# Two groups of heads scored in one TensorE stage, in three of the five attention mixers of a float32 transformer kernel

## The reference, cut to what matters

```python
# differential attention (layers 0 and 3): 8 heads, each with two score maps j = 0, 1 of 64 dimensions
s = jnp.einsum('bqhjd,bkhjd->bhjqk', qb, k) * scale + bias
s = jnp.where(dist >= 0, s, NEG)
p = jax.nn.softmax(s, axis=-1)
a = p[:, :, 0] - lam_full * p[:, :, 1]
o = jnp.einsum('bhqk,bkhe->bqhe', a, v)

# stick-breaking attention (layer 1): 16 heads of 64 dimensions
z = jnp.einsum('bqhd,bkhd->bhqk', qb, k) * scale
log_1m_beta = jnp.where(strict, jax.nn.log_sigmoid(-z), 0.0)
between = lax.cumsum(log_1m_beta, axis=3, reverse=True) - log_1m_beta
a = jnp.where(strict, jnp.exp(jax.nn.log_sigmoid(z) + between), 0.0)

# block attention with ALiBi (second block): 8 heads of 64 dimensions; with 256 tokens
# a query sees its own block alone, so this is causal attention over all keys
p = jax.nn.softmax(where(kpos <= qpos, q @ k.T - slopes * (qpos - kpos), -inf), axis=-1)
# beside it, on the other half of the channels
y = jnp.einsum('bsgc,gcd->bsgd', trailing_mean(p_in) - p_in, pool_w)
```

## Time and profile before

| what | us |
|---|---|
| median of 3 runs | 1755.77 (1755.76 to 1756.32) |
| span of the profiled execution | 1753.6 |
| what lies around the span in the runs (median less span) | 2.2 |
| TensorE busy, matmuls | 1744.2 (99%) |
| VectorE busy | 1301.7 (74%) |
| ScalarE busy | 1059.2 (60%) |
| GpSimd busy | 97.1 (6%) |

### The profile page before, as it was taken

The page is one execution under the profiler, slowest core; times in us unless marked ns, Lnnn a source line. Parts: engine busy times, 40 slices in busy tenths (PEclk is TensorE's granted clock), DMA queues, the critical chain, the costliest instruction groups (busy, mean ns, idle before and its releaser), DMA issues.

```text
span 1753.6 us, 33156 instructions
## 1 busy us (share of the span) xinstructions
PE 1744.2 (99%) x13030; PEld 1646.4 (94%) x13030; DVE 1301.7 (74%) x1899; ACT 1059.2 (60%) x1592; POOL 97.1 (6%) x144
## 2 busy tenths in 40 slices
PE   9999999999999999999999999999999999999998
PEld 8999999999999999999999999999999999998887
DVE  7668878877877886877876697788666876556665
ACT  6776566666666666666666766566454555346444
POOL 3000000122000013000000000003000020000000
PEclk9999999999999999999999999999999999999999
DMA  9445555534566544565554465655555544435652
GB/s 310 147 145 168 193 191 159 190 133 138 176 203 190 180 170 146 170 214 181 180 179 145 146 192 192 187 183 193 192 180 195 161 164 139 161 127 189 201 178 96
DMA packets 238483, 306.27 MB, mean 175 GB/s; under 512 B 13763, under 2 KB 212981, under 8 KB 238333
## 3 DMA queue, kind: packets, MB, share of 16 engines
q1 hardware_dynamic: 236708, 300.27, 52.5%
q0 software_dynamic: 1552, 4.28, 0.7%
q10 hardware_dynamic: 104, 0.07, 0.0%
HBM read 303.53 MB, written 1.07 MB: 174 GB/s over the span
## 4 chain that ended last, share of the span: by engine, by line
PE 99%; DVE 0%; ACT 0%; issue 0%; DVEq 0%; POOL 0%; POOLq 0%; ACTq 0%
PE ps L1111 22%; PE ps L1112 22%; PE ps L1113 22%; PE ps L1467 17%; PE ps L1469 9%; PE ps L1278 1%; PE ps L1298 1%; PE ps L1625 0%; PE ps L1124 0%; PE ps L1328 0%; PE ps L1315 0%; PE ps L1270 0%; PE ps L1395 0%; PE ps L1353 0%; PE ps L1386 0%; PE ps L1367 0%
## 5 line engine op out<-in xcount | busy, mean ns | idle before, releaser
L1683 DVE TENSOR_TENSOR sb_w_lo<-sb_raw,sb_w_hi 128x2048 fp32r<-128x2048 f32 x283 | 646.0, 2290 | 225.4 <-ACT sb_w_hi L907 224.6
L907 ACT ACTIVATE sb_w_hi<-sb_raw 128x2048 fp32r<-128x2048 f32 x283 | 538.5, 1908 | 160.5 <-PE ps L1113 78.7
L1111 PE MATMUL ps<-sb_a_hl,sb_w_hi 128*128 128x256 f32 x1840 | 529.3, 288 | 1.8 <-DVE sb_a_hl L1697 1.0
L1112 PE MATMUL ps<-sb_a_hl,sb_w_hi 128*128 128x256 f32 x1840 | 520.4, 283 | 0.0
L1113 PE MATMUL ps<-sb_a_hl,sb_w_lo 128*128 128x256 f32 x1840 | 520.2, 283 | 0.0
L1467 PE MATMUL ps<-sb_a_hl,sb_w_hi 128*128 128x512 f32 x1280 | 447.6, 393 | 0.0
L1111 PEld LDWEIGHTS ps<-sb_a_hl,sb_w_hi 128*128 128x128 f32 x1840 | 352.2, 191 | 9.8 <-issue 6.4
L1469 PE MATMUL ps<-sb_a_hl,sb_w_lo 128*128 128x256 f32 x1280 | 358.2, 280 | 0.0
L1112 PEld LDWEIGHTS ps<-sb_a_hl,sb_w_hi 128*128 128x128 f32 x1840 | 352.5, 192 | 0.4
L1113 PEld LDWEIGHTS ps<-sb_a_hl,sb_w_lo 128*128 128x128 f32 x1840 | 352.4, 192 | 0.0
L1467 PEld LDWEIGHTS ps<-sb_a_hl,sb_w_hi 128*128 128x128 f32 x1280 | 239.7, 187 | 53.2
(11 more groups left out here) (264 smaller groups left out, 1908.9 us busy)
## 6 DMA issues: line engine op xcount, KB each, us to landing
sb_raw<-in_ffn_w_up SPq DMA_DIRECT2D x102, 1024.0 KB, 5.3
sb_raw<-in_ffn_w_down SPq DMA_DIRECT2D x66, 1024.0 KB, 4.9
sb_raw<-in_da_w_qkv SPq DMA_DIRECT2D x23, 1024.0 KB, 5.2
sb_raw<-in_ffn_w_gate SPq DMA_DIRECT2D x22, 1024.0 KB, 5.3
sb_raw<-in_w_o SPq DMA_DIRECT2D x16, 1024.0 KB, 5.0
sb_raw<-in_sb_w_qkv SPq DMA_DIRECT2D x12, 1024.0 KB, 5.2
sb_raw<-in_xa_wkv SPq DMA_DIRECT2D x8, 1024.0 KB, 5.4
sb_raw<-in_w_in SPq DMA_DIRECT2D x8, 1024.0 KB, 5.4
```

The source lines that it names most:

```text
L907: act.activation(w_hi[:, a % RING, :], raw[:, a % RING, :], ACT.Copy).then_inc(hi_ready, 1)
L1111: pe.matmul(o, hi1, hi2, start=start, stop=False, skip_group_check=True)
L1112: pe.matmul(o, hi1, lo2, start=False, stop=False, skip_group_check=True)
L1683: dve.tensor_tensor(w_lo[:, a % RING, :], raw[:, a % RING, :], w_hi[:, a % RING, :].bitcast(F32), ALU.subtract).then_inc(lo_ready, 1)
```

## The change

- `mix` on TensorE calls `scores` or `stick_scores` for groups g and g+1 one after the other, at the half where group g stood, for g = 0, 2, 4, 6 (differential, stick-breaking) or 0, 2 (block attention). The half that had group g+1 loses that stage. Sliding-window and cross attention stay as they are.
- Two groups need room: the wide part of group g goes to half g % 2 of bank 4 + head, the narrow part to a quarter of bank 2 + head (`score_tile`). `copy_scores` on VectorE thus becomes two instructions. VectorE waits for the scores of both groups before it reads the first.
- Bank 2 is no longer one of the projections': in these forms blocks 0, 1, 2 go to banks 0, 1, 6, and the rest turns over banks 0 and 1 (`proj_bank`), so block i waits for block i-2 to be taken. The norm's sum and its turned root move to bank 7.
- Bank 3 is now shared between narrow scores and what it held: `pool_mix(0)` waits for `biased` of groups 0 and 1; `back(0)` and the early `stick_values` wait for the first four groups to be read; the pair that starts with group 4 (group 2 in block attention) waits for `act_lo` to reach 4. The first output block begins with banks 2 and 3.
- The convolution's setup transposes move from banks 5 and 6 to 2 and 3.

```diff
+        def proj_bank(form, i):
+            if form in ("slide", "cross"):
+                return i % 3
+            return (0, 1, 6)[i] if i < 3 else (i - 3) % 2
+        def score_tile(form, g, s, wide_part):
+            if form == "slide":
+                return PS[:, 4 + s, P:3 * P] if wide_part else PS[:, 4 + s, 0:P]
+            if wide_part:
+                return PS[:, 4 + s, g % 2 * T:(g % 2 + 1) * T]
+            return PS[:, 2 + s, g % 2 * P:(g % 2 + 1) * P]
...
-                            pe.wait_ge(taken, ph["tk"] + i - 2)
+                            pe.wait_ge(taken, ph["tk"] + freed_block(form, i) + 1)
...
-                    if g >= 1:
+                    if g >= 1 and (form == "slide" or g % 2 == 0):
                         pe.wait_ge(biased, ph["sg"] + g)
+                    if form == "diff" and g == 4 or form == "moba" and g == 2:
+                        pe.wait_ge(act_lo[a], 8 * ph["out_fill"] + 4)
...
                         pe.wait_ge(rT_ready, rT_count[ph["n"]])
+                        pe.wait_ge(biased, ph["sg"] + 2)
...
-                        if h in at["scores"]:
+                        if h in at["scores"][::2]:
                             scores(at["scores"].index(h))
+                            scores(at["scores"].index(h) + 1)
...
-                    dve.wait_ge(scores_ready, sg + 1)
+                    dve.wait_ge(scores_ready, sg + (2 - g % 2 if form in ("diff", "moba") else 1))
...
-                    dve.wait_ge(z_done, g + 1)
+                    dve.wait_ge(z_done, g + 2 - g % 2)
...
-                    dve.tensor_scalar(of_group(zbuf, g), PS[:, 4:6, 0:3 * P], ph["scale"], None, ALU.mult)\
-                        .then_inc(z_copied, 1)
+                    z = of_group(zbuf, g)
+                    dve.tensor_scalar(z[:, :, 0:T], PS[:, 4:6, g % 2 * T:(g % 2 + 1) * T], ph["scale"], None,
+                                      ALU.mult)
+                    dve.tensor_scalar(z[:, :, T:3 * P], PS[:, 2:4, g % 2 * P:(g % 2 + 1) * P], ph["scale"], None, ALU.mult)                        .then_inc(z_copied, 1)
```

More of the change, by code:

```diff
@@ L414, in value_bank, with freed_block, root_bank, turned_root @@
             return 4 + g % 2
+        def proj_bank(form, i):
+            if form in ("slide", "cross"):
+                return i % 3
+            return (0, 1, 6)[i] if i < 3 else (i - 3) % 2
+        def freed_block(form, i):
+            return next(e for e in range(i - 1, -1, -1) if proj_bank(form, e) == proj_bank(form, i))
+        def root_bank(form):
+            return 3 if form in ("slide", "cross") else 7
+        def turned_root(form):
+            return DB[3][:, T:T + QB] if form == "slide" else PS[:, 7, 0:QB]
+        def score_tile(form, g, s, wide_part):
[4 more added lines that the diff above has]
+            return PS[:, 2 + s, g % 2 * P:(g % 2 + 1) * P]
         def heads_of(form, g):
@@ L1194, in project @@
                             pe.wait_ge(act_lo[ph["act"]], 8 * ph["fill"] + k + 1)
-                        o, first, js = PS[:, i % 3, j * T:(j + 1) * T], (j, k) == (0, 0), slice(j * P, (j + 1) * P)
+                        o, first, js = PS[:, proj_bank(form, i), j * T:(j + 1) * T], (j, k) == (0, 0), slice(j * P, (j + 1) * P)
                         if typ == "mv":
@@ L1230, in out_half @@
                     elif i == 0:
-                        order = [(k, m) for p in (2 * half, 2 * half + 1) for k in range(2) for m in (2 * p, 2 * p + 1)]
+                        pairs_of = (2 * half, 2 * half + 1) if form in ("slide", "cross") else ((2, 3), (1, 0))[half]
+                        order = [(k, m) for p in pairs_of for k in range(2) for m in (2 * p, 2 * p + 1)]
                     else:
@@ L1238, in out_half @@
                             pe.wait_ge(act_lo[a], 8 * ph["out_fill"] + arrival(form, c) + 1)
-                        if i == 0 and k == 0 and m in (0, 2, 4):
-                            pe.wait_ge(taken, ph["tk"] + max(n for n in range(N) if n % 3 == m // 2) + 1)
+                        if i == 0 and k == 0 and m == 4 and form == "stick":
+                            pe.wait_ge(z_copied, 8)
+                        elif i == 0 and k == 0 and m == 4 and form in ("diff", "moba"):
+                            pe.wait_ge(biased, ph["sg"] + ph["groups"])
+                        elif i == 0 and k == 0 and m in (0, 2, 4):
+                            pe.wait_ge(taken, ph["tk"] + max(n for n in range(N) if proj_bank(form, n) == m // 2) + 1)
                         if i == 0 and k == 0 and m == 6 and form in ("slide", "moba", "cross"):
@@ L1377, in stick_values @@
                     pe.wait_ge(a_ready, g + 1)
-                    if bank > 3:
-                        pe.wait_ge(z_copied, 8)
+                    pe.wait_ge(z_copied, 8 if bank > 3 else 4)
                     before = [e for e in range(g) if value_bank("stick", e) == bank]
@@ L1455, in mix @@
                             turn_probs(at["turn"].index(h))
-                        if h in at["scores"]:
+                        if form == "moba" and h in at["scores"][::2]:
+                            scores(at["scores"].index(h))
+                            scores(at["scores"].index(h) + 1)
+                        elif form != "moba" and h in at["scores"]:
                             scores(at["scores"].index(h))
```

38 lines of the change are left out of this document (22 added, 16 removed).

## The result

The change made the kernel slower by 0.13%, less than the 0.2% that I had said a measurement can tell; the interval of the ratio lies above 1.

The account below looks back on a forecast made before the run. TensorE was taken to bound the kernel. Fourteen joins at 0.40 us gain 5.6; waits of 2.5, 2.8 and 0.95 give +0.65, so the median goes from 1755.8 to 1756.4 us, range 1752.4 to 1759.5.

Parts of the forecast that it names:

- What bounds the kernel: TensorE, busy 1744.2 of 1753.6 us; only its own work and waits it does not have today can move the time.
- the 0.40 for leaving the 128-row form: Each second score group, put behind the first, saves 0.40 us of going from 128 rows to 64 and back.
- The gain of stick-breaking attention, 4 x 0.40: Four score pairs in stick-breaking attention each save 0.40 us, as the join of two groups is taken as free.
- The wait for `maxima(1)`, 2.5: Block attention's pooling stage on TensorE waits 2.5 us for VectorE, which does `maxima(1)` behind a 2.29 us low part.
- The two waits for `out_lo(3)`, 2 x 1.4: Scores of group 4 in each differential attention wait 1.4 us, as VectorE does `out_lo(3)` behind two low parts; 2.8 us together.
- `suffix`, 0.95 in all (0.55, 0.15, 0.15 to 0.25, 0.05): In stick-breaking attention TensorE's `suffix` waits for `t_lo` at groups 2, 4, 6 and 0; 0.95 us, between 0 and 3.2.
- Projections on two banks: nothing: Block i waits for the take of block i-2; cost 0, with 3 us to spare.
- The sum, +0.65: Whole kernel: -5.6 + 2.5 + 2.8 + 0.95 = +0.65 us, a median of 1756.4 us.
- The rival of open gates: VectorE or ScalarE reach `maxima(1)` and `out_lo(3)` earlier, so the whole 5.6 us gain stays: 1750.2 us; chance 0.10.
- The rival of the clock, 0.04: The pooling wait lowers TensorE's granted clock for one block of 48 products: +5.8 us, 1762.1 us; chance 0.04.
- more waits: Stick-breaking's four pairs and differential attention's eight each cost 0.4 us more in waits: +4.8, 1761.2 us; chance 0.05.
- a join that costs half: Joining two score groups costs half of the 0.40 us, so the gain is 2.8 us: 1759.2 us; chance 0.05.

Follow-up runs that it names:

- heads in step: The changed kernel with stick-breaking score matmuls reordered, both heads' wide parts, then both heads' narrow parts: 1758.69 us, ratio 1.0012.
- stick apart: The changed kernel, but in stick-breaking attention each group's scores are issued at their own half again: 1758.75 us, ratio 1.0015.
- `out_lo` first: The changed kernel, but in differential attention one weight block's low and high parts are made after `out_lo(3)` and `out_hi(3)`: 1754.88 us, ratio 0.9995.
- wait alone: The kernel before, with its first pooling stage also waiting for a low part that VectorE finishes 2 us later: 1759.73 us, ratio 1.0019.
- differential apart: The changed kernel, but in both differential attentions each group's scores are issued at their own half again: 1761.9 us, ratio 1.0034.

## Why the prediction was right, and where it was not

- **What bounds the kernel, and the 0.40 for leaving the 128-row form.** Right. Differential and block attention gave 0.39 a pair in after, and taking it back gave 3.1 us for eight pairs. By the Trainium skill (TensorEngine Tiling (Array Packing), Key Properties), a change of the tiling mode drains the engine, a change of tile alone does not; the ten pairs agree with it, at 1.51 us for 0.86 + 0.65.
- **The gain of stick-breaking attention, 4 x 0.40.** Mis-sized: 4 x 0.28. The step that failed is "within a group the two heads already alternate with nothing but the passes' own time left over". It holds within a group, but not across the join, where one head comes a narrow pass late. With each size of both heads issued side by side the join is free here too (0.39). I had taken the prices of both mixers from rows but overlooked that `stick_scores` issues its matmuls in another order than `scores`. That the order does it is measured; how the array hands out the passes is not.
- **The wait for `maxima(1)`, 2.5.** Right: 2.42 of idleness, 2.7 in the trace where the clock stays up. VectorE was late by its own queue; scores that came one half sooner did not start it sooner.
- **The two waits for `out_lo(3)`, 2 x 1.4.** Right in kind and nearly in size: the gap is 1.42, and the trace moves by 1.5 at each. Taking them away gave 2.9.
- **`suffix`, 0.95 in all (0.55, 0.15, 0.15 to 0.25, 0.05).** Right in sum: 0.56, 0.19, 0.21 and none. The reasoning from slack held, but in after two of its terms missed and cancelled. For group 2 TensorE came 0.27 sooner, not 0.40, since the join gave less; and the copy waited for a pair that was 0.1 longer, so that `t_lo` ended 0.49 later, not 0.4. With the heads in step both terms are as predicted, 0.39 and 0.40, and the wait is the same.
- **Projections on two banks: nothing.** Right; no product waits for `taken`.
- **The sum, +0.65.** It should have been +1.6 by the places alone: 0.47 more from the stick joins, 0.2 from `out_lo`, 0.2 at the pooling stage, 0.1 from the differential joins. That gives 1757.4, the lowest level. That the median lies only 1.0 above the number is in part luck: in 11 of 21 executions the clock did not add its 1.5.
- **Two sums in the text.** Waits between 0.6 and 1.2 of the 6.25 us summed give 1753.9 to 1757.7, not 1752.6 to 1759; the measured median lies inside the narrower range too. The rival of open gates at 1750.2 leaves out the 0.95 at `suffix`; with it the time would be 1751.1.
- **The rival of the clock, 0.04.** Its direction was right and its chance far too low: 10 of 21 executions lie above the lowest level, the profiled one among them, with the clock down, which was also a sign of being wrong that I had named. The size was too high: I priced it at 5.8 us for a whole block, and it costs 1.4 to 1.6, since only 3.4 us pass at the lower level. It did not make the median slower than my range, but four executions lie above the range's upper end. The argument against it was that the clock outlasted 3 us of idleness at the end. That was one trace: over the ten profiles the fall at the end comes from 2.0 to 5.1 us after TensorE's last matmul, so the end of one program says little of a wait of 2.4 us. The Trainium skill (TensorE: Matmul & The Clock Gate, HAM oscillation), by which idle gaps between bursts of matmuls send the clock down, was right in the direction where I doubted it. The gaps that it warns of are longer than this one, though, and here the measurement decides: 2.42 us and 2.0 us were enough in most executions.
- **The rivals of open gates, of more waits, and of a join that costs half.** The first two did not come: all the new waits found in the trace are those I had summed. The third came in part, in stick-breaking attention alone, where a join costs 0.12 of the 0.20 that I had priced.

What stays open: nothing here tells why the same 2.42 us wait brings the clock down in one execution and not in the next.

Why the executions above the lowest fall in two levels (1.2 and 2.2 us above it) is answered in part. Each of the five profiles with a low clock at this place has one such stretch, of 3.41 us, priced at 1.4 to 1.6, so the upper level needs no second fall. The profiles differ in their first 15 us, which last longer than in the trace of before by 0 (after), 0.15 (stick apart), 0.6 (heads in step), 0.9 (`out_lo` first) and 1.05 (wait alone). These profiled executions lie 1.3, 1.3, 2.1, 1.95 and 2.25 us above the lowest of their kernels. The longer first 15 us thus go with the upper level. That this holds for the executions without a profile is not shown.

## What to carry to other kernels

Joining two short stages saves the change of array form once, but it also draws the second one's gates forward: list, for each gate, what stands ahead of the releaser on its engine, and move that as part of the same change. Here joins worth 5.0 us were paid for with 5.7 at three waits on VectorE's order, 1.0 at `suffix`, and often 1.5 of low clock; reordering VectorE and ScalarE at these places, and the heads of the stick-breaking scores, turned the same joins into a gain of 3.9. On the evidence of this one kernel, a wait of 2 us on a TensorE that is otherwise full should be priced above its length, and matmuls that nobody reads can fill it.

## What the runs showed of the hardware that I had not expected

- **Clock.** In the profile with the wait alone TensorE had worked at full clock, stood idle for 2.0 us and worked on for 0.75 us; then its granted clock was at the lower level (1.2 GHz) for 3.4 us. 8 of 11 executions of that kernel have the time that goes with it. After an idle 2.4 us it fell in four of the five profiles that have that wait (after, no `out_lo` waits, heads in step, stick apart) and stayed up in one (differential apart). After 1.4 us, which six profiles have twice each, it never fell.
- **The fall can come after the idleness.** Counted from the end of the last matmul before the wait, the clock went down after 2.0 (`out_lo` first), 2.4 (heads in step), 2.7 (wait alone) and twice 3.7 us (after, stick apart). In the last three TensorE was already at work again.
- **Executions.** Over the six kernels with an idle 2.0 or 2.4 us there, 42 of 71 executions lie at their kernel's upper levels, and 32 of these have a mean clock of 0.998, but none of the other 29. In the three kernels with the wait removed or filled, and in before, none of 33 and 61 has it.
- **Price.** The stretch at the lower level lasted 3.41 us each time. At the same wait of 2.42 us, the four traces with it take 1.4 to 1.6 us more at that place than the one without (differential apart).
- **Two heads in separate rows of the array** do not stay in step by themselves. With each head's wide and narrow matmuls issued one behind the other, two groups in a row took 1.61 us; with both heads' wide ones first, 1.51.
